# x transposed on the host, the first norm applied behind the projection, and the first loads in four contiguous pieces

## What is computed

```python
def rmsnorm(x, w):
    xf = x.astype(jnp.float32)
    y = xf * lax.rsqrt(jnp.mean(xf * xf, axis=-1, keepdims=True) + EPS)
    return (y * w.astype(jnp.float32)).astype(x.dtype)
...
        h = rmsnorm(x, norm1_w[l])
        proj = jnp.einsum('bsd,dp->bsp', h, w_in[l])
        (aq, ak, av, z, xbc, dt_raw, m_qk, m_v, m_o, m_i, m_f) = split_columns(proj, PROJ_SIZES)
        aq = rmsnorm(aq.reshape(head_shape), q_norm_w[l])
        ak = rmsnorm(ak.reshape(head_shape), k_norm_w[l])
        y_att = moba_attention(aq, ak, av.reshape(head_shape))
        y_ssm = mamba2_ssd(z, xbc, dt_raw, ...)
        y_mlstm = mlstm_chunkwise(m_qk, m_v, m_o, m_i, m_f, ...)
        x = x + jnp.einsum('bsm,md->bsd', mix, w_out[l])
        h = rmsnorm(x, norm2_w[l])
        x = x + conv_glu(h, ffn_w_up[l], ffn_conv_w[l], ffn_conv_b[l], ffn_w_down[l])
```

## Time and profile before

| | |
|---|---|
| median of 3 runs | 424.66 us (424.19 to 424.69) |
| profiled execution | 423.99 us, span of its instructions 422.1 us |
| PE | busy 409.3 us, 2677 matmuls |
| DVE, ACT, POOL | busy 284.8, 247.1, 37.6 us |
| DMA | 73.60 MB, mean 174 GB/s |

### The profile page before, as it was taken

One profiled execution on the slowest core, in us unless ns is written; L12 is line 12 of the kernel. 1 busy time (PEld: TensorE's weight loads), 2 busy tenths in 40 slices (PEclk: granted clock), 3 DMA queues, 4 the chain that ended last, 5 costly groups with the idle time before them and its releaser, 6 DMA issues.

```text
span 422.1 us, 6708 instructions
## 1 busy us (share of the span) xinstructions
PE 409.3 (97%) x2677; PEld 369.6 (88%) x2677; DVE 284.8 (67%) x399; ACT 247.1 (59%) x331; POOL 37.6 (9%) x28
## 2 busy tenths in 40 slices
PE   2999999999999999999999999999999999999996
PEld 2999999778888887677888999999999999999995
DVE  3888797756756678688645866574765655757663
ACT  4868877794388666997635564443454544434540
POOL 2522444410011000000000000000000000000000
PEclk9999999999999999999999999999999999999999
DMA  7755793445362442225543365445455554454202
GB/s 262 293 196 192 264 328 143 162 158 221 130 235 104 160 138 99 99 101 200 199 177 123 118 259 220 166 158 200 177 199 199 191 194 156 168 196 188 101 0 99
DMA packets 11581, 73.60 MB, mean 174 GB/s; under 512 B 1300, under 2 KB 1448, under 8 KB 3368
## 3 DMA queue, kind: packets, MB, share of 16 engines
q1 hardware_dynamic: 11560, 73.30, 47.5%
HBM read 72.23 MB, written 1.07 MB: 174 GB/s over the span
## 4 chain that ended last, share of the span: by engine, by line
PE 94%; ACT 2%; DMA 2%; issue 0%; SPq 0%; DVE 0%; DVEq 0%; ACTq 0%
PE pj L1203 24%; PE pj L1205 24%; PE pj L1204 24%; PE mx L1257 5%; PE mx L1203 5%; PE mx L1204 5%; PE mx L1205 5%; PE mx L1254 3%; DMA wraw<-in_w_in 2%; ACT whi L380 1%; ACT seg_b L522 0%; ACT L507 0%; ACT L522 0%; ACT xdt_b L529 0%; DVE x_sb L1194 0%
## 5 line engine op out<-in xcount | busy, mean ns | idle before, releaser
L758 DVE TENSOR_TENSOR wlo<-wraw,whi 128x2048 fp32r<-128x2048 f32 x58 | 132.7, 2289 | 74.2 <-ACT whi L380 74.2
L380 ACT CAST whi<-wraw 128x2048 fp32r<-128x2048 f32 x63 | 119.7, 1903 | 74.7 <-PE pj L1205 74.7
L1203 PE MATMUL pj<-hT_hi,whi 128*128 128x256 f32 x512 | 145.4, 284 | 0.6 <-DVE hT_lo L777 0.6
L1205 PE MATMUL pj<-hT_hi,wlo 128*128 128x256 f32 x512 | 144.9, 283 | 0.0
L1204 PE MATMUL pj<-hT_lo,whi 128*128 128x256 f32 x512 | 144.9, 283 | 0.0
L1203 PEld LDWEIGHTS pj<-hT_hi,whi 128*128 128x128 f32 x512 | 98.0, 191 | 1.5 <-DVE hT_lo L777 0.8
L1204 PEld LDWEIGHTS pj<-hT_lo,whi 128*128 128x128 f32 x512 | 98.0, 191 | 0.4
L1205 PEld LDWEIGHTS pj<-hT_hi,wlo 128*128 128x128 f32 x512 | 98.0, 191 | 0.0
L1203 PE MATMUL pj<-whi,hT_hi 128*128 128x512 f32 x144 | 58.2, 404 | 0.0
L1205 PE MATMUL pj<-whi,hT_lo 128*128 128x512 f32 x144 | 56.3, 391 | 0.0
L1204 PE MATMUL pj<-wlo,hT_hi 128*128 128x512 f32 x144 | 56.1, 390 | 0.0
(11 more groups left out here) (212 smaller groups left out, 441.4 us busy)
## 6 DMA issues: line engine op xcount, KB each, us to landing
wraw<-in_w_in SPq DMA_DIRECT2D x23, 1024.0 KB, 4.9
wraw<-in_w_up SPq DMA_DIRECT2D x22, 1024.0 KB, 4.8
wraw<-in_w_down SPq DMA_DIRECT2D x11, 1024.0 KB, 4.8
wraw<-in_w_out SPq DMA_DIRECT2D x8, 1024.0 KB, 4.8
seg_b<-ld_rows SPq DMA_DIRECT2D x4, 512.0 KB, 5.7
x_sb<-in_x SPq DMA_DIRECT2D x2, 512.0 KB, 3.6
wraw<-in_w_in SPq DMA_DIRECT2D x4, 256.0 KB, 6.7
Wm_b<-m_rows_d SPq DMA_DIRECT2D x1, 512.0 KB, 7.0
```

The lines of the kernel that those rows point to most:

```text
L380: nc.scalar.copy(whi[:, slot, :], wraw[:, slot, :]).then_inc(s.hi_done, 1)
L758: nc.vector.tensor_tensor(wlo[:, slot, :], wraw[:, slot, :], whi[:, slot, :].bitcast(F32), ALU.subtract).then_inc(s.lo_done, 1)
L1203: pe_mm(ps, a_hi, b_hi, start=start, stop=False, skip_group_check=shared)
L1205: return pe_mm(ps, a_lo, b_hi, start=False, stop=stop, skip_group_check=shared)
```

## The change

**Host.** `xt` is x transposed (channel on the partition, 8 blocks of 256 tokens), with norm1_w in eight columns before it, cut into `xt0` and `xt1`. Unit 0 is stored as `w0`, two halves of 128 x 1024. All four are contiguous pieces of 512 KB. x itself is loaded as well, later.

**Start.** ACT multiplies the blocks of xt by norm1_w into `hT_hi` (`x_hi`), DVE gives `hT_lo` (`x_lo`), with no norm in them. PE's 16 transposes and the scaling of x's rows are gone. `first_unit` orders unit 0's products by quarter and part, so that PE can begin on the first cast quarter. Units 0, 1 and 2 are all split in quarters by ACT and DVE, none by POOL.

**The norm.** ACT and DVE sum x's squares while PE works, and DVE makes diag(1/rms) of 128 x 128 for each half. `spread_r1` on PE, after the first quarter of unit 2, multiplies it by ones: every partition gets the row of 1/rms. DVE copies it to `rbc`. For the convolution groups the new `conv_scale(g)` multiplies PSUM by `rbc` in place, before `conv_base`. For the small projection one multiply stands ahead of `rows_softplus`. The other groups have tokens on the partitions, so ACT's evacuation takes 1/rms as its scale, in two halves instead of one operation; for q and k it goes into the heads' factors.

**Order.** small_proj goes from slot 0 to 2, cols_turn from 4 to 6, xs_turn from 6 to 7; rows_softplus, rows_scans, rows_dec, cols_copy on DVE from 0, 2, 3, 5 to 3, 4, 5, 6; xs_evac from 7 and 9 to 8 and 9; ACT's rows_softplus and rows_exps from 0 and 3 to 3 and 5. SP issues x after unit 2, `par` and `w24` after unit 3.

```diff
+            n = KD + 4 * T
+            sp.dma_start(xn_b[:, 0:n], A["xt0"][:, :]).then_inc(s.xt_in0, 16)
+            sp.dma_start(wraw[:, 0, 0:1024], A["w0"][0:P, :]).then_inc(s.w0_in0, 16)
+            sp.dma_start(xn_b[:, n:], A["xt1"][:, :]).then_inc(s.xt_in1, 16)
+            sp.dma_start(wraw[:, 0, 1024:2048], A["w0"][P:2 * P, :]).then_inc(s.w0_in1, 16)
+            for u in range(1, U_OUT):
+                if u == 3:
+                    sp.dma_start(x_sb[:, 0, :], A["x"][0, 0:P, :]).then_inc(s.x_in0, 16)
+                    sp.dma_start(x_sb[:, 1, :], A["x"][0, P:T, :]).then_inc(s.x_in1, 16)
+                if u == 4:
                     sp.dma_start(par[:, :], A["par"][:, :]).then_inc(s.par_in, 16)
-            sp.dma_start(w24, A["w24"].rearrange("p (k n) -> p k n", k=KD)).then_inc(s.w24_in, 16)
+                    sp.dma_start(w24, A["w24"].rearrange("p (k n) -> p k n", k=KD)).then_inc(s.w24_in, 16)
...
             def conv_base(g, b):
 
-                group_computed(g)
+                act.wait_ge(s.conv_in, 2 * g + b + 1)
...
+            def x_hi(k):
+
+                act.wait_ge((s.xt_in0, s.xt_in1)[k // 4], 16)
+                nc.scalar.activation(hT_hi[:, k, :], xT[:, k, :], ACT.Copy, scale=n1[:, k:k + 1]).then_inc(s.hi_T, 1)
...
+                link(nc.vector.tensor_tensor(small, bank[0][0:68, 0:T], rbc[0:68, :], ALU.mult))
...
+            def conv_scale(g):
+
+                dve.wait_ge(s.unit_done, 2 * g + 2)
+                for b in range(2):
+                    v = pj[g % 2][:, 512 * b:512 * (b + 1)].rearrange("p (k t) -> p k t", k=2)
+                    nc.vector.tensor_tensor(v, v, rbc[:, :].unsqueeze(1).to_broadcast([P, 2, T]), ALU.mult).then_inc(s.conv_in, 1)
...
-            at(0, rows_softplus)
+            at(3, rows_softplus)
+            first_at(1, conv_scale, 0)
             for g in range(NCONV):
+                if g:
+                    at(2 * g + 2, conv_scale, g)
                 for b in range(2):
                     at(2 * g + 2, conv_taps, g, b)
-            at(2, rows_scans)
-            at(3, rows_dec)
-            at(5, cols_copy)
+            at(4, rows_scans)
+            at(5, rows_dec)
+            at(6, cols_copy)
             for c in range(NT):
                 for half in range(2):
-                    at(7 + 2 * c, xs_evac, c, half)
+                    at(8 + c, xs_evac, c, half)
...
+            def spread_r1():
+
+                pe.wait_ge(s.consts, 4)
+                pe.wait_ge(s.rd1_ready, NT)
+                for t in range(NT):
+                    ins = mm(bank[1][:, t * P:(t + 1) * P], ones[:, :], rdiag[:, t, :])
+                ins.then_inc(s.rb1_ps, 1)
...
+                if u == 0:
+                    first_unit(pj[0]).then_inc(s.unit_done, 1)
+                elif u == 1:
+                    channels_first(pj[0], 1, 1, s.lo_T, s.w1_lo).then_inc(s.unit_done, 1)
+                elif u == 2:
+                    channels_first(pj[1], 2, 0, pieces=s.w2_lo, between=spread_r1, where=1).then_inc(s.unit_done, 1)
```

More of the change, by code:

```diff
@@ L467, in seg_exp, with rstd @@
                                              bias=cols[:, C_LD[c] + 4 * j + h:C_LD[c] + 4 * j + h + 1]).then_inc(s.seg_exp, 1)
+            def rstd(c):
+                return stat[:, 2 + c:3 + c]
             def mv_copy():
                 group_computed(G_MV)
-                nc.scalar.copy(vaug[:, :, :, 0:P],
-                               pj[G_MV % 2][:, :].rearrange("p (c h d) -> p c h d", c=NT, h=MH)).then_inc(s.mv_ready, 1)
+                for c in range(NT):
+                    nc.scalar.activation(vaug[:, c, :, 0:P], pj[G_MV % 2][:, c * 512:(c + 1) * 512].rearrange("p (h d) -> p h d", h=MH),
+                                         ACT.Copy, scale=rstd(c)).then_inc(s.mv_ready, 1)
             def cst_copy():
@@ L484, in qk_square @@
                 group_computed(g)
-                nc.scalar.activation(qk_rows[:, g - G_AQ, :], pj[g % 2][:, :], ACT.Square).then_inc(s.qk_sq, 1)
+                for c in range(NT):
+                    cs = slice(c * 512, (c + 1) * 512)
+                    nc.scalar.activation(qk_rows[:, g - G_AQ, cs], pj[g % 2][:, cs], ACT.Square, scale=rstd(c)).then_inc(s.qk_sq, 1)
             def qk_root(i):
@@ L1205, in products, with first_unit, channels_first @@
                 return pe_mm(ps, a_lo, b_hi, start=False, stop=stop, skip_group_check=shared)
-            def channels_first(ps, slot, half, turned=None, pieces=None, between=None):
+            def first_unit(ps):
+                for k in range(4):
+                    pe.wait_ge(s.hi_T, k + 1)
+                    pe.wait_ge(s.w0_hi, k + 1)
+                    for c in range(4):
+                        nc.tensor.matmul(ps[:, c * T:(c + 1) * T], whi[:, 0, k * 512 + c * P:k * 512 + (c + 1) * P], hT_hi[:, k, :],
+                                         start=k == 0 and c % 2 == 0, stop=False, skip_group_check=True)
+                    pe.wait_ge(s.lo_T, k + 1)
+                    for c in range(4):
+                        nc.tensor.matmul(ps[:, c * T:(c + 1) * T], whi[:, 0, k * 512 + c * P:k * 512 + (c + 1) * P], hT_lo[:, k, :],
+                                         start=False, stop=False, skip_group_check=True)
+                    pe.wait_ge(s.w0_lo, k + 1)
+                    for c in range(4):
+                        ins = nc.tensor.matmul(ps[:, c * T:(c + 1) * T], wlo[:, 0, k * 512 + c * P:k * 512 + (c + 1) * P], hT_hi[:, k, :],
+                                               start=False, stop=False, skip_group_check=True)
+                return ins
+            def channels_first(ps, slot, half, turned=None, pieces=None, between=None, where=2):
                 for k in range(4):
                     kk = half * 4 + k
-                    if k == 2 and between:
+                    if k == where and between:
                         between()
@@ L1445, in at @@
                 jobs.setdefault(slot, []).append((job, args))
-            at(0, small_proj)
-            at(4, cols_turn)
-            at(6, xs_turn)
+            at(2, small_proj)
+            at(6, cols_turn)
+            at(7, xs_turn)
             at(9, bc)
```

183 lines of the change are left out of this document (95 added, 88 removed).

## The result

The changed kernel takes **426.57 us** (median, 425.90 to 432.92) where the kernel before takes 424.44 beside it: a ratio of 1.0047, with a 95% interval from 1.0039 to 1.0054. It is slower, by 2.1 us, and the forecast was 5.2 us slower. The ratio leaves out one disturbed execution, the 432.92, which is taken up under e11_as_changed.

A forecast was written before the change was run, and what follows sets the result against it. The prediction took PE, busy 97% of the span, as the bound, made to wait by DVE's chain. It summed 1.2 (chain), 3.3 (DVE beside POOL) and 0.7 (slow PE) to 5.2 us later, 424.66 + 5.2 = 429.9, range 424.6 to 434.5.

The forecast's parts named there:

- Here POOL is first by 0.3 us: Near unit 11, POOL's subtraction for unit 12 was to start 0.3 us before DVE's split(11), with 4.3 to go.
- +3.3 for DVE: Term for DVE's split(11) being slowed beside POOL's subtraction for unit 12: 3.3 us on DVE's chain.
- +0.7 of clock behind the longer wait: Term for PE running slow after standing idle 4.4 us before state(): 0.7 us.
- +1.2: Unit 11 starts at 84.3, 1.2 us later than before, the 3.45 earlier start being spent on PE's waits.
- the DVE chain alone: Rival: DVE's chain delays unit 11 with no meeting with POOL, total 425.9; chance 0.25.
- C: Forecast time at which DVE's cols_copy ends, 58.8; later steps up to unit 11 are counted from it.
- DVE loses 77% of the time beside POOL: Rate for DVE's split(11) behind POOL's subtraction: 0.66 us lost of 0.86 in one row.
- The 1.6: Term for PE's slow stretch at the start, now paid by the first projection: 1.6 us, between 0 and twice that.
- this stretch is no new cost: Rival: the first projection matmuls ran slow before as well, so the end is 1.6 earlier, 428.3; chance 0.03.
- DVE's chain: DVE's jobs one behind the other from 21.4 to the end of cols_copy: together 37.4 us.
- The faster rival: PE keeps its start, 421.2, if rbc to unit 11 is over 1.2 shorter than 62.9 us; chance 0.15.
- The split at unit 4: DVE's split(3) starts at 22.6, POOL's subtraction of unit 4 at 24.5; rival with POOL first there: 433.4, chance 0.15.

The follow-up runs named there:

- e11_as_changed: The changed kernel run again unchanged, timed beside the kernel before: 426.74 us, ratio 1.0047.
- e5_nudge: Changed kernel plus one unused DVE copy of 256 columns from PSUM ahead of split(11), so POOL's subtraction starts first: 433.01 us, ratio 1.0198 to the kernel before.
- e2_warm: Changed kernel plus nine float32 matmuls on a tile of ones on PE ahead of the first unit: 426.44 us, ratio 1.0040 to the kernel before.
- e6_bc_first: Changed kernel with ACT's bc_copy moved ahead of group 4's base, DVE order untouched: 426.87 us, ratio 1.0048 to the kernel before.
- e3_no_scale: Changed kernel without conv_scale, so the convolved groups lack 1/rms and ACT's base waits for the unit: 428.07 us, ratio 1.0077 to the kernel before.
- e1_xs_early: Changed kernel with DVE's xs_evac of the first rows moved ahead of group 3's taps: 422.74 us, ratio 0.9953 to the kernel before.
- e12_all_no_scale: Changed kernel with xs_evac, cols_copy and bc_copy earlier, nine warming matmuls, third and fourth loads swapped, no conv_scale: 421.02 us, ratio 0.9911 to the kernel before.

## Why the prediction was wrong in size

**The step that failed is "Here POOL is first by 0.3 us".** The +3.3 for DVE, and the +0.7 of clock behind the longer wait, stood on it. In the trace the two operations begin 0.01 us apart and POOL pays. Without these terms the forecast's own sum was 84.3 at unit 11, +1.2, and the total 425.9, the rival "the DVE chain alone", which it named with 0.3 us as the margin. The mechanism itself held: e5_nudge has that lead, and DVE pays there.

The lead was lost on POOL's side. Both starts were counted from C, so that C came 1.2 later moved both alike. DVE's split came at C + 15.67 for 15.7. POOL's subtraction came at C + 15.66 for 15.4: PE was done with unit 9 at C + 13.60 for 13.4, and the hand-overs from PE to the cast (0.09) and from the cast to POOL (0.07) had no term. (The rounded terms as printed give 15.8 and 15.3, so the margin was no better known than 0.2 either.) Nor was it luck of one execution. In all four traces with this order on DVE (the changed kernel, e11_as_changed, e2_warm, e6_bc_first) the recorded starts are within 0.02 us, now POOL's first, now DVE's, and DVE loses nothing. That DVE has the better of such a tie is what four traces show, not a thing that the forecast could have known; each end should have had its price.

Even with the lead the sum would have been short: 429.9 against the 433.0 of e5_nudge. The loss was 4.1 for 3.3. And the lower clock behind the long wait cost more than 0.7: state() took 3.8 us there and 2.0 in e11_as_changed, with more lost behind it (0.50 up to 92).

**The size of the loss was wrong too.** "DVE loses 77% of the time beside POOL" came from one short operation. In three runs it lost 4.14 of 4.26, 4.26 of 4.38 and 2.09 of 2.24, all but 0.12 to 0.15 us. The old row fits this: the same addition took 1.23 when DVE had it first (at 98.05 in the changed kernel), so of the 0.86 beside POOL it lost 0.71, again all but 0.15. A fixed remainder had been read as a share. The Trainium skill, "SBUF — State Buffer", Who interferes with whom, has the rule: who issues first has the shared ports for the whole instruction, and the other is blocked. By it the loss would be 4.3; the trace agrees, within 0.15. The prediction had set it aside for the one row.

**The slow first stretch has no fixed price.** It cost 2.55 in the profiled execution, where the sum had 1.6. The 1.6 was taken from the transposes of before, inside the bound "between 0 and twice that". There the stretch was over with the transposes, after 3.3 us of PE's work; here it took in 26 matmuls at 0.21, 5.5 us. In the nine traces with this start it cost 1.4 to 2.8, 1.4 in e11_as_changed, so the 1.6 lies within, near the low end. What sets its length stays open. With PE starting 0.4 later (6.33 for 5.9: the first half of w0 was used at 5.56 for 5.3, and a hand-over of 0.14 was not counted), the row of 1/rms was copied to the end of 22.9 instead of 21.4. The prediction's rival that this stretch is no new cost is refuted: before, the projection's matmuls were 0.12 apart right behind the transposes, and here they are 0.21 apart for as long as the stretch lasts.

**DVE's chain was right.** From the first scaling to the end of cols_copy it took 37.1 us (22.94 to 60.03) for 37.4; conv_scale, which no row had shown, took 1.30 for two, the price of the read. The taps of group 3 started at C + 6.9 for 7.0, xs_evac(0) was done at C + 15.8 for 15.7, PE waited 2.3 for 2.3, and the bc copy ended at C + 23.7 for 23.8. But e3_no_scale shows that up to cols_copy a chain without the scalings takes as long, since DVE then waits for ACT. The forecast had the right length, and took it for DVE's alone.

**The clock behind the 2.3 us wait was costed at nothing.** The 0.7 was set on a wait of 4.4. Here 2.3 us sufficed in most executions, and PE reached state() at 84.38, 0.7 after the bc copy was there (83.70). The terms then close: +1.2 as forecast, +1.2 for C at 60.0 instead of 58.8, +0.6 for the slow stretch, together 3.0 for the 2.98 measured. In e11_as_changed, with the clock up, they are +1.2 as forecast, +0.7 for C at 59.5, and 0.2 from C on, for 2.08.

**The faster rival** said that it decides if the chain is shorter than 62.9 by over 1.2. It was 63.2, from 22.90 to 86.10, the slow stretch in it. But reordering alone (e1_xs_early) brought 3.8 us, because the chain had time in it in which DVE waited for ACT. The prediction names that time ("in the old kernel xs_evac of the first rows ran during this wait") but its rivals all keep the order. e12_all_no_scale, without the ten scalings, is where PE's waits after its start shrink to 1.2 us and the old one at the attention, and it is 3.6 us under the kernel before (with the warm start and the mended order in it). The split at unit 4 went to DVE, as forecast: POOL took 5.45 there and nobody waited.

## What to carry to other kernels

An earlier start is worth only what the engines behind it can keep. Put the added work on the chain that feeds the bound engine, and follow that chain over every engine that it crosses, here DVE and ACT. Look in it first for time in which an engine waits: reordering gained 3.8 us once, where a job went into such time, and afterwards only moved the wait from one job to the next. Where two DVE and POOL operations that read SBUF tensors start within a few tenths of a microsecond, cost both outcomes, keep them apart by order, and distrust an experiment that shifts them against each other. Profile the same kernel twice before a difference between two traces is put down to an edit: here cols_copy ended 0.5 us apart in two traces of one kernel.

## What was not expected

- The outcome of a meeting between DVE and POOL turns on less than 0.2 us: POOL 0.01 ahead by the record lost 2.1 and DVE nothing; POOL 0.18 ahead lost nothing and DVE 4.3. Less work on the chain (e3_no_scale) was slower for it.
- Behind the same wait of 2.3 us PE's granted clock fell in one trace (0.50 from 78 to 80) and stayed at 1.00 in others (e11_as_changed, e2_warm). Of the executions of the changed kernel some have a mean of 0.999 or 1.000 and a span of 423.8 to 424.2, most 0.995 or 0.996 and 424.2 to 425.4: the fall costs about half a microsecond, since without it PE waits 1.0 us at state().
- Matmuls on a constant tile during the idle start brought the full rate forward (four matmuls in 0.64 us at 6.95, where the changed kernel took 1.05 at 7.32), at no cost to the first unit, and the total did not move (426.44 for 426.57).
